# Squared-ReLU MLP of a three-block model on one Trainium2 core: where two down blocks are multiplied, and where the x forms and the pair loads stand

## The reference, cut to what matters

```python
def first_block(x, ...):
    h = x
    for layer in range(DEPTH):                      # 2 layers: stick-breaking attention, then retention
        h = h + mixer(rms_norm(h, g_mix[layer]))
        h = h + squared_relu_mlp(rms_norm(h, g_mlp[layer]), w_mlp_up[layer], w_mlp_down[layer])
    return rms_norm(h, g_final)

def squared_relu_mlp(h, w_up, w_down):              # 512 tokens, D_MODEL 1024, MLP_HIDDEN 4096
    u = jax.nn.relu(h @ w_up)
    return (u * u) @ w_down
```

## Time and profile before

| | |
|---|---|
| median of 3 runs | 2537.36 us (2537.24 to 2539.12) |
| profiled execution, own time | 2546.55 us |
| span of its profile | 2544.7 us |
| mean granted TensorE clock | 0.989 |
| PE busy | 2474.6 us (97%) |
| DVE busy, ACT busy | 1532.9 us (60%), 1073.1 us (42%) |
| DMA | 97 GB/s over the span |

### The profile page before, as it was taken

How to read it: one execution, slowest core, us unless ns; L and a number is a source line. 1 busy time by engine, 2 the same in 40 slices (tenths; PEclk the granted TensorE clock), 3 DMA queues, 4 the chain that set the end, 5 groups by cost and what they waited for, 6 DMA issues and landing times.

```text
span 2544.7 us, 33902 instructions
## 1 busy us (share of the span) xinstructions
PE 2474.6 (97%) x12552; PEld 2075.5 (82%) x12552; DVE 1532.9 (60%) x2120; ACT 1073.1 (42%) x1517; POOL 125.8 (5%) x111
## 2 busy tenths in 40 slices
PE   9999888989999999989999999999999999999999
PEld 7888778978888888778888888888878778888887
DVE  5877746646667765566556544544777856544343
ACT  3776525435333443444345432222455444323222
POOL 2001100000100000200000300000100000000000
PEclk9999899999999999999999999999999999999999
DMA  4111335333322222344353232233322212223323
GB/s 142 52 57 61 124 106 149 112 103 125 100 75 75 91 75 83 127 121 126 99 148 92 91 105 95 94 99 99 99 75 67 75 59 100 97 93 99 99 91 115
DMA packets 84156, 247.83 MB, mean 97 GB/s; under 512 B 13136, under 2 KB 23632, under 8 KB 83920
## 3 DMA queue, kind: packets, MB, share of 16 engines
q1 hardware_dynamic: 75776, 229.58, 27.1%
q0 software_dynamic: 4032, 14.68, 3.4%
q10 hardware_dynamic: 4240, 2.10, 0.3%
HBM read 244.23 MB, written 2.10 MB: 97 GB/s over the span
## 4 chain that ended last, share of the span: by engine, by line
PE 85%; DVE 5%; DMA 4%; issue 2%; ACT 2%; POOL 1%; SPq 0%; DVEq 0%; ACTq 0%; POOLq 0%
PE ps L2477 41%; PE ps L2482 20%; PE ps L2820 4%; DMA forms<-in_stream 4%; PE ps L2824 2%; PE ps L2837 2%; PE ps L3146 2%; PE ps L2546 2%; PE ps L2889 1%; PE ps L2530 1%; PE ps L2701 1%; PE ps L2658 1%; PE ps L2677 1%; PE ps L2642 1%; PE ps L2876 1%
## 5 line engine op out<-in xcount | busy, mean ns | idle before, releaser
L708 ACT ACTIVATE w_hi<-raw 128x1024 fp32r<-128x1024 f32 x350 | 371.1, 1060 | 1018.8 <-PE ps L2482 926.0
L2477 PE MATMUL ps<-x_hi,w_hi 128*128 128x512 f32 x1488 | 588.0, 395 | 0.0
L2477 PE MATMUL ps<-x_lo,w_hi 128*128 128x512 f32 x1488 | 580.3, 390 | 0.0
L1455 DVE TENSOR_TENSOR w_lo<-raw,w_hi 128x1024 fp32r<-128x1024 f32 x350 | 430.7, 1231 | 111.3 <-ACT w_hi L708 111.0
L2482 PE MATMUL ps<-x_hi,w_lo 128*128 128x512 f32 x1488 | 367.6, 389 | 0.0
L2477 PEld LDWEIGHTS ps<-x_hi,w_hi 128*128 128x128 f32 x1488 | 280.1, 188 | 62.8 <-issue 4.0
L2477 PEld LDWEIGHTS ps<-x_lo,w_hi 128*128 128x128 f32 x1488 | 280.1, 188 | 58.3 <-issue 1.7
L2482 PEld LDWEIGHTS ps<-x_hi,w_lo 128*128 128x128 f32 x1488 | 279.3, 188 | 58.1
L2477 PE MATMUL ps<-u_hi,w_hi 128*128 128x512 f32 x794 | 309.5, 390 | 1.1 <-ACT w_hi L708 1.1
L2477 PE MATMUL ps<-u_lo,w_hi 128*128 128x512 f32 x794 | 309.0, 389 | 0.0
L2482 PE MATMUL ps<-u_hi,w_lo 128*128 128x512 f32 x794 | 196.7, 389 | 0.0
(11 more groups left out here) (454 smaller groups left out, 3828.3 us busy)
## 6 DMA issues: line engine op xcount, KB each, us to landing
raw<-in_stream SPq DMA_DIRECT2D x357, 512.0 KB, 3.3
forms<-in_stream SPq DMA_DIRECT2D x56, 512.0 KB, 4.5
forms<-in_stream POOLq DMA_DIRECT2D x28, 512.0 KB, 5.5
forms<-in_stream SPq DMA_DIRECT2D x28, 256.0 KB, 5.5
x_tok<-in_x SPq DMA_DIRECT2D x4, 512.0 KB, 7.6
out_x<-xn ACTq DMA_DIRECT2D x7, 256.0 KB, 2.3
tab_ret<-in_tables_ret SPq DMA_DIRECT2D x1, 1536.0 KB, 6.5
raw<-in_stream SPq DMA_DIRECT2D x3, 256.0 KB, 3.3
```

Of the source, the lines that this page charges most:

```text
L708: nc.scalar.activation(w_hi[:, slot(n)], raw[:, slot(n)], ACT.Copy).then_inc(hi_done, 1)
L1455: nc.vector.tensor_tensor(w_lo[:, slot(n)], raw[:, slot(n)], w_hi[:, slot(n)].bitcast(F32), ALU.subtract).then_inc(lo_done, 1)
L2477: nc.tensor.matmul(ps[:, gemm_bank(n)], w_hi[:, s, k], x(k), start=(k == 0 and i == 0), stop=False)
```

## The change

- **PE.** `of_new_u` is gone. `down_part(n, made, chunks)` multiplies some chunks of a down block into its open bank. The first down block takes chunks 0 to 3 before the last two units of the up phase, (last,4) and (last,3), and chunks 4, 5 after them; then the second down block takes chunks 0 to 5, and both take chunk 6, then chunk 7.
- **DVE and ACT at the end of an up phase.** The last two units leave the loop, and what belongs to them is written out in another order: `up_low` of the pair before goes ahead of `third_form` of the next group, and `form_high` of the next group's third unit (v + 4) goes to the end.
- **Pair loads.** `load_forms` has four loads, each with a wait and a semaphore group of its own: `a_in` (for units 1 and 2), `r_in` (two halves, for the accumulating load), `b_in` (unit 3). Raw loads of the third and fourth down block stand ahead of them.
- **x forms.** Turn 1 is made at the end of the product before and in dense block 0, and turns 2 and 3 in dense blocks 0 to 2. `x_fp` lies elsewhere, so only the third `form_high` waits for the last `x_forms_low`. `fourth_form` comes after the dense blocks. `form_slot` starts at slot 0 in each layer.

```diff
@@ SP
-                block = up_block_at(q)
-                if q % UP_PAIRS < 2:
+                block, into, early = up_block_at(q), forms[q % 2], q % UP_PAIRS < 2
+                if early:
                     sp.wait_ge(mm_done, RUN_AT[("mlp0", "mlp1")[q // UP_PAIRS]] + 2 + 1)
                 else:
+                    sp.wait_ge(*upto("f_sum", 2 * (q - 2) + 2))
+                    sp.wait_ge(*upto("f_lo", UNIT_AT[q - 2, 2] + 1))
+                sp.dma_start(into[:, 0:2].rearrange("p a f -> p (a f)"), stream[block]).then_inc(flag(f"a_in_{q % 2}"), 16)
+                if not early:
+                    sp.wait_ge(*upto("f_lo", UNIT_AT[q - 2, 5] + 1))
+                sp.dma_start(into[:, 2], stream[block, :, 0:T]).then_inc(flag(f"r_in_{q % 2}"), 16)
+                if not early:
+                    sp.wait_ge(*upto("f_lo", UNIT_AT[q - 2, 7] + 1))
+                sp.dma_start(into[:, 3], stream[block + 1, :, 0:T]).then_inc(flag(f"r_in_{q % 2}"), 16)
+                if not early:
                     sp.wait_ge(*upto("f_lo", UNIT_AT[q - 2, 3] + 1))
-                into = forms[q % 2]
-                sp.dma_start(into[:, 0:2].rearrange("p a f -> p (a f)"), stream[block]).then_inc(flag(f"r_in_{q % 2}"), 16)
-                sp.dma_start(into[:, 3:5].rearrange("p a f -> p (a f)"), stream[block + 1]).then_inc(flag(f"r_in_{q % 2}"), 16)
-                sp.dma_start(into[:, 2], stream[block, :, 0:T]).then_inc(flag(f"r_in_{q % 2}"), 16)
+                sp.dma_start(into[:, 4], stream[block + 1, :, T:2 * T]).then_inc(flag(f"b_in_{q % 2}"), 16)
...
                 for g in range(len(MLP_GROUPS)):
+                    n = first + UP_DENSE + DC * g + 2
+                    load(n)
+                    load(n + 1)
                     qs = sorted({q for q, _ in up_phase(layer, g)})
...
@@ ACT, ahead_of_norm
-                    if k in (N_MLP0, N_MLP1) and c >= 4:
-                        x_scaled(k, c - 4)
-                    if k in (N_MLP0, N_MLP1) and c >= 5:
-                        x_forms_high(k, c - 5)
+                    if k in (N_MLP0, N_MLP1) and c == 4:
+                        x_scaled(k, 0)
+                    if k in (N_MLP0, N_MLP1) and c == 6:
+                        x_forms_high(k, 0)
+                        x_scaled(k, 1)
@@ ACT, up_pairs, after the loop over all but the last two units
+                q, v = qs[-1], first + len(units) - 2
+                positive(layer, q - 1, 2)
+                squared(q - 1, 1)
+                up_high(layer, q - 1, 1)
                 positive(layer, q, 1)
+                if v + 3 < end:
+                    form_high(v + 3)
+                positive(layer, q, 0)
                 squared(q, 0)
                 up_high(layer, q, 0)
                 positive(layer, q, 2)
                 squared(q, 1)
                 up_high(layer, q, 1)
+                if v + 4 < end:
+                    form_high(v + 4)
@@ ACT, mlp, dense blocks c = 0..3
                     if c == 0:
+                        x_forms_high(norm, 1)
                         root(norm)
-                    if c == 1:
-                        x_scaled(norm, 3)
                     if c == 3:
-                        act.wait_ge(*upto("xs_lo", 4 * layer + 4))
-                        for v in range(layer * len(UNITS) // 2, layer * len(UNITS) // 2 + 3):
-                            form_high(v)
+                        form_high(layer * len(UNITS) // 2)
+                        form_high(layer * len(UNITS) // 2 + 1)
...
                     if c in (1, 2):
                         x_forms_high(norm, c + 1)
+                    if c < 2:
+                        x_scaled(norm, c + 2)
+                act.wait_ge(*upto("xs_lo", 4 * layer + 4))
+                form_high(layer * len(UNITS) // 2 + 2)
@@ DVE, residual_of_norm
-                    if k in (N_MLP0, N_MLP1) and c >= 6:
-                        x_forms_low(k, c - 6)
-                    if k in (N_MLP0, N_MLP1) and c >= 5:
-                        x_forms(k, c - 5)
+                    if k in (N_MLP0, N_MLP1) and c == 5:
+                        x_forms(k, 0)
+                    if k in (N_MLP0, N_MLP1) and c == 6:
+                        x_forms_low(k, 0)
...
                 sum_low(k)
                 if k in (N_MLP0, N_MLP1):
-                    x_forms_low(k, 1)
+                    x_forms(k, 1)
@@ DVE, up_pairs, after the loop over all but the last two units
+                q, v = qs[-1], first + len(units) - 2
+                more = v + 2 < end
+                fourth_sum(layer, q)
+                up_low(layer, q - 1, 0)
+                if more:
+                    form_low(v + 2)
+                up_low(layer, q - 1, 1)
+                if more:
+                    third_form(q + 1)
+                    form_low(v + 3)
+                third_sum(q)
+                up_low(layer, q, 0)
+                up_low(layer, q, 1)
+                if more:
+                    fourth_form(q + 1)
@@ DVE, mlp, dense blocks
-                    if c in (1, 2):
+                    if c < 3:
                         x_forms_low(norm, c + 1)
-                    if c in (0, 1):
+                    if c < 2:
                         x_forms(norm, c + 2)
+                fourth_form(layer * UP_PAIRS)
@@ PE
+            def down_part(n, made, chunks):
+
+                pe.wait_ge(sig("ul_done"), made + chunks[-1] + 1)
+                for i, (w, x) in enumerate(((w_hi, u_hi), (w_hi, u_lo), (w_lo, u_hi))):
+                    for k in chunks:
+                        last = nc.tensor.matmul(ps[:, gemm_bank(n)], w[:, slot(n), k], x[:, 0, k],
+                                                start=(k == 0 and i == 0), stop=(k == KC - 1 and i == 2))
+                if chunks[-1] == KC - 1:
+                    last.then_inc(mm_done, 1)
...
-                    for unit in up_phase(layer, g):
+                    made = layer * HIDDEN // P + KC * g
+                    units = up_phase(layer, g)
+                    for unit in units[:-2]:
                         up_unit(UNIT_AT[unit])
-                    of_new_u(n, layer * HIDDEN // P + KC * g)
-                    dense(n + 1, lambda k: u_hi[:, 0, k], lambda k: u_lo[:, 0, k])
+                    weights_of(n)
+                    down_part(n, made, range(4))
+                    for unit in units[-2:]:
+                        up_unit(UNIT_AT[unit])
+                    down_part(n, made, range(4, 6))
+                    weights_of(n + 1)
+                    down_part(n + 1, made, range(6))
+                    for k in (6, 7):
+                        down_part(n, made, (k,))
+                        down_part(n + 1, made, (k,))
```

More of the change, by code:

```diff
@@ L106 @@
            "x_sum": ("abs_b_done", 16), "xs_hi": ("oh_done", 8), "xs_lo": ("ol_done", 8), "down_scaled": ("qkl_done", 16),
-           "r_in_0": ("x_in_2", 16), "r_in_1": ("x_in_3", 16)}
+           "r_in_0": ("x_in_2", 16), "r_in_1": ("x_in_3", 16), "a_in_0": ("x_in_0", 16), "a_in_1": ("x_in_1", 16),
+           "b_in_0": ("ident_in", 16), "b_in_1": ("gain_in", 16)}
 RUN_AT, N_RUN = {}, 0
@@ L337, in build @@
         assert where[0] <= top - T * 4
-        x_fp = sb("x_fp", [P, 2, T], over=ring_at)
+        x_fp = sb("x_fp", [P, 2, T], over=sq_new_at)
         x_sum = sb("x_sum", [P, 4, HALF], over=ring_at + 2 * T * 4)
@@ L532, in form_of, with form_slot @@
             return form_sum[:, (6, 4).index(p)] if p in (6, 4) else forms[q % 2][:, (1, 2, 5, 7, 3).index(p)]
+        def form_slot(v):
+            return v % (len(UNITS) // 2) % FORM_SLOTS
         def up_bank(q, p):
@@ L654, in load_mlp @@
                             load_forms(q + 2)
-                    n = first + UP_DENSE + DC * g + 2
                     if g + 1 < len(MLP_GROUPS):
-                        load_run(n, n + DC - 2)
+                        load_run(n + 2, n + DC - 2)
                         load(n + DC - 2)
@@ L907, in form_high @@
                 else:
-                    act.wait_ge(*upto(f"r_in_{q % 2}", 48 * (q // 2 + 1)))
+                    act.wait_ge(*upto(f"{'b' if p == 3 else 'a'}_in_{q % 2}", 16 * (q // 2 + 1)))
                 if v >= FORM_SLOTS:
-                    act.wait_ge(*upto("f_mm", v - FORM_SLOTS + 1))
-                nc.scalar.activation(form_hi[v % FORM_SLOTS], form_of(q, p), ACT.Copy).then_inc(flag("f_hi"), 1)
+                    act.wait_ge(*upto("f_mm", max(v - FORM_SLOTS + 1, v - v % (len(UNITS) // 2))))
+                nc.scalar.activation(form_hi[form_slot(v)], form_of(q, p), ACT.Copy).then_inc(flag("f_hi"), 1)
             def copy_of(q, p):
@@ L960, in up_pairs @@
                 qs = sorted({q for q, _ in units})
-                for v in range(first, first + len(units)):
+                for v in range(first, first + len(units) - 2):
                     q, p = UNITS[v]
@@ L981, in up_pairs @@
                         up_high(layer, q - 1, 1)
-                    if p == 7 and q == qs[-1] and q > qs[0]:
```

(28 more changed lines are left out.)

6 lines of the change are left out of this document (3 added, 3 removed).

## The result

The changed kernel takes 2481.33 us (median of 4 runs, 2480.03 to 2481.90) against 2537.3 us of the kernel before on the same chip: ratio 0.9779, 95% interval 0.9762 to 0.9796. The forecast was 2477, range 2468 to 2495. In the profiled executions the step is larger, 2546.55 to 2481.90 us, 64.6 instead of the 60.3 of the sum; in the timed runs it is 56.0.

The account below looks back on a forecast made before the run. PE, busy 97% of the span, was taken as the bound, with idle waits and half-clock stretches to win. 28.0 + 11.2 + 7.2 + 5.6 + 1.1 + 13.0 - 5.8 = 60.3 us gave 2477 us, range 2468 to 2495.

Parts of the forecast that it names:

- The end of the up phases: After T, the end of PE's unit (last,7): 28.0 us of `u_lo` waits and 11.2 us of clock go.
- Were it as late as now: Accumulating load landing at T + 6.5: chunks 6 and 7 ready at T + 9.0 and T + 10.9, still in time.
- The loads: Pair loads split, raw loads moved ahead: `second_copy` waits, 7.2 us, and the late weight block, 1.1 us, go.
- The seam: New PE wait where the third down block needs the first one's slot: 0.73 us, eight times, 5.8 us given back.
- The head: Start of each layer's MLP: first `form_high` ends 6.5 us sooner, 13.0 us over two layers; bounds 7.8 and 16.
- The size of the sum: Whole kernel: all gains less the seams give 60.3 us, from the profiled 2546.55 us to 2486.3.
- I take the same 60.3 from it: The profiled gain is also taken from the median, 9.2 us lower than the profiled execution, giving 2477 us.
- (1): Eight idle stretches at the seams lower PE's clock: price 13.6 us, 2491 us; chance 0.08.
- (2): Layer head gives nothing, as moved x forms lengthen the chain to the first unit: price 13.0, 2490 us; chance 0.12.
- (3): Up-phase end: wait moves to chunks 6 and 7, half of 28.0 + 11.2 us left: 2497 us; chance 0.07.
- (4): Up phases: pair loads come too late throughout, one wait per pair, 27 us slower: 2564 us; chance 0.03.
- (5): Up phases: the loads change nothing and `second_copy` stays, 7.2 us: 2484 us, inside the main case's range.

Follow-up runs that it names:

- late_loads: The changed kernel with all four pair loads behind the last wait as before, and the raw loads of the third and fourth down block behind them: 2490.78 us.
- order_alone: The changed kernel with late pair and raw loads and PE's order as before, leaving the new order on DVE and ACT: 2487.57 us.
- before_again: The kernel before, with no edit, profiled once more: median 2538.3 us of ten runs, profiled execution 2541.82 us.

## Why the prediction was right, point by point

*The end of the up phases.* Right in each place: chunk 5 at T + 2.8 (forecast T + 3.1), 6 at T + 6.8 (6.8), 7 at T + 8.9 (8.9); wanted at T + 5.5, 10.9, 12.3. The whole 28.0 us and the clock went. But the prediction credited the end as one piece. The runs show that PE's interleave, the part that looks like the change, adds nothing in this form once order and loads are there (2480.5 without it), since what it gives on `third_copy` the seam takes. One size was off without harm: the accumulating load was to come 4.4 us sooner (T + 2.1), and came 9.0 us sooner (T - 2.4).

*"Were it as late as now"*: with the interleave DVE's order covers a late load; late_loads shows 0.6 us of `u_lo` waits in all, with the latest landing at T + 5.9. Without the interleave a landing at T + 6.5 cost 2.0 us (order_alone).

*The loads.* `second_copy` and the late raw block went. That block was under-rated. The prediction put the raw loads' new place at 1.1 us, what the block waited before; in late_loads it waits 4.0 us and is the larger part of the loss. It hangs on the table load, which waits for chunk 7, and the interleave makes chunk 7 later: without the new place of the raw loads the interleave costs time (late_loads is 3.2 us slower than order_alone).

*The seam.* Forecast 0.73 us of PE each, measured 0.71 start to start (0.55 by the profile's idle time). Right, term by term: 0.39 + 0.03 + 1.06 + 0.14 = 1.62 us against the forecast 1.65; the 0.04 "before it", which the prediction took from no row, came out at 0.03. Finishing the blocks in turn gives it back.

*The head.* Forecast 6.5 us a layer, measured 35.2 - 28.3 = 6.9 and, in layer 1, 6.8. Wait left about 6.4 forecast, 5.9 measured.

*The size of the sum.* Against the profile 64.6 instead of 60.3. The traces split it so: the heads gave 13.7 instead of 13.0, the groups (from a layer's first unit on) 52.3 instead of 47.3, and the changed kernel came to block 0 of layer 0 1.4 us later (267.78 against 266.43), which no part of the change explains. Of the 5.0 us in the groups 3.6 are what the seam showed, an estimate from its 0.15 us: each of the 24 waits on `u_lo`, `second_copy` and `third_copy` of the earlier trace rows cost that much more than its listed idle time. The other 1.4 stay open.

Against the timed runs it is 56.0 instead of 60.3. Here the step that was too large is "I take the same 60.3 from it": the profiled execution of before was 9.2 us above its median, and its long `u_lo` waits were not those of a usual execution (before_again shows 6.2 us less of them). The prediction had named this as what could shorten the gain. That the forecast came within 4.3 us is in part luck: waits priced too low made up for half of what the slow profile added.

*The rivals.* (1) The eight seams lower the clock: they ran at 1.00, as the windows up to and behind group 0's seam show, and the ten us behind each of the other seven are at 1.00 too; only the heads lie at half. The Trainium skill, "TensorE: Matmul & The Clock Gate", section "A second HAM failure mode: psum-queue depth-cycling", tells of short idle stretches in each iteration that bring the clock down. Here there is one in about 85 us (330.06 to 414.80), so the runs neither bear the rule out nor speak against it. (2) The head gives nothing: 10.5 us in two separate pairs of kernels. (3) The tail's wait moves on: no, slack is 4.2 and 3.4 us. (4) Loads late in every pair: no wait for a load reaches PE in the up phases. (5) The loads change nothing: no, `second_copy` is off the list.

## What to carry to other kernels

When a wait has several causes in a row (a late transfer, finished work queued behind the instruction that needs it, a consumer that comes early), each remedy alone looks large and the last one added looks like nothing; try them in combinations before keeping the most intricate. A remedy that looks like nothing may also be paying for a new wait of its own: the interleave gave 5.6 us once its seam was mended. Two blocks that are finished in alternation end together, and whatever refills their slot is then exposed: finish them in turn. Moving work in front of a wait whose end does not come sooner pushes the half-clock stretch onto what follows. And when a load is late, look at what stands ahead of it in its queue: here it was the load of a table that had nothing to do with the phase.

## What the runs showed of the hardware that was not expected

Accumulating loads of the same program land at times that differ by some 4 us from execution to execution (the wait behind one was 6.70 us in one profile and 2.89 in another). The kernel before, which waits for them, has runs spread over up to 19 us (2530.24 to 2549.05 in 15 runs); every version with early loads stays within 2 us (2480.03 to 2481.90 in the changed kernel), and so does late_loads, where the loads are late but PE hardly waits for them (2490.39 to 2491.24).

The idle time of TensorE before a matmul understates what the wait cost by about 0.16 us a wait, the part of the last matmul that overlaps with its successor: a matmul of 512 columns is listed with 0.39 us, and the next begins 0.23 us after it.
